# A two-layer decoder trunk on one core: halves for branch 0 and for the next layer made sooner, four p projections inside the first PLE gate tile, the first pair's head sums after half a matmul tile

## What is computed

```python
for i in range(DEPTH):                                   # DEPTH = 2
    xn = rmsnorm(h, norm_mix[i])
    q, k, v, cb, cc, cu, pu, gate_logits = split(xn @ w_in[i])
    att  = stick_breaking_attention(rmsnorm(q), rmsnorm(k), v)     # 8 heads x 64
    conv = cb * causal_short_conv(cc * cu, conv_w[i])
    pool = causal_pool_mixer(pu, pool_w[i]) * pool_scale[i]
    branch_d = einsum('bsjc,jcd->bsjd', stack([att, conv, pool]), w_branch[i])
    h = h + sum_j(sigmoid(gate_logits_j) * branch_d_j) @ w_out[i]
    h = h + peer_ffn(rmsnorm(h, norm_ffn[i]), ...)       # 16384 one-neuron experts, 8 heads x top 16
    h = h + sigmoid(rmsnorm(h, norm_ple[i]) @ w_ple_gate[i]) * (p[i] @ w_ple_proj[i])
```

## Time and profile before

| | us |
|---|---|
| runs | 3905.82, 3909.05, 3908.99 |
| median | 3908.99 |
| profiled execution, its own time | 3910.81 |
| span of that profile | 3909.0 |
| PE busy | 3828.8 (98% of the span) |
| DVE busy | 2878.5 (74%) |
| ACT busy | 1450.8 (37%) |
| POOL busy | 1474.3 (38%) |
| mean granted TensorE clock | 0.992 of full speed |

### The profile page before, as it was taken

One profiled execution on the slowest core, in us unless ns is written; L12 is line 12 of the kernel. 1 busy time (PEld: TensorE's weight loads), 2 busy tenths in 40 slices (PEclk: granted clock), 3 DMA queues, 4 the chain that ended last, 5 costly groups with the idle time before them and its releaser, 6 DMA issues.

```text
span 3909.0 us, 53929 instructions
## 1 busy us (share of the span) xinstructions
PE 3828.8 (98%) x17258; PEld 3140.4 (80%) x17258; DVE 2878.5 (74%) x4061; ACT 1450.8 (37%) x1957; POOL 1474.3 (38%) x935
## 2 busy tenths in 40 slices
PE   8999999999999999999999999999999999999997
PEld 5777888888888878888767778888888887888886
DVE  6753658989997287788577536599899963888785
ACT  5533333333333333333444333333333333333334
POOL 1100003444444277666101000045444443777651
PEclk9999999999999999999999999999999999999998
DMA  3222223445554699999222223234455546999991
GB/s 114 70 86 97 92 92 123 144 172 189 187 188 175 209 357 360 358 352 342 102 69 77 85 93 101 88 131 145 172 194 192 189 165 231 370 361 352 351 330 70
DMA packets 323770, 740.36 MB, mean 189 GB/s; under 512 B 30497, under 2 KB 161697, under 8 KB 319905
## 3 DMA queue, kind: packets, MB, share of 16 engines
q1 hardware_dynamic: 104400, 381.73, 28.1%
q10 hardware_dynamic: 174160, 222.40, 16.6%
q0 software_dynamic: 45056, 134.38, 9.3%
HBM read 618.87 MB, written 119.54 MB: 189 GB/s over the span
## 4 chain that ended last, share of the span: by engine, by line
PE 95%; DVE 2%; issue 1%; ACT 1%; DMA 1%; POOL 0%; DVEq 0%; ACTq 0%; POOLq 0%; SPq 0%
PE banks L1218 62%; PE banks L1434 26%; PE banks L1413 2%; PE banks L1280 1%; PE banks L1270 1%; PE banks L1288 1%; PE banks L1360 0%; ACT hi L453 0%; PE banks L1265 0%; DVE xl L787 0%; DMA vrow<-in_stream,tail_v 0%; DVE lo L775 0%; DMA raw<-in_stream 0%; ACT xh L469 0%; DVE xl L956 0%
## 5 line engine op out<-in xcount | busy, mean ns | idle before, releaser
L1218 PE MATMUL banks<-xh,hi 128*128 128x512 f32 x3264 | 1293.1, 396 | 27.1 <-DVE xl L787 18.5
L1218 PE MATMUL banks<-xl,hi 128*128 128x512 f32 x3264 | 1276.0, 391 | 0.0
L1218 PE MATMUL banks<-xh,lo 128*128 128x512 f32 x3264 | 1273.7, 390 | 0.0
L401 POOL TENSOR_TENSOR lo<-raw,hi 128x1024 fp32r<-128x1024 f32 x240 | 646.0, 2692 | 984.0 <-ACT hi L453 983.8
L775 DVE TENSOR_TENSOR lo<-raw,hi 128x1024 fp32r<-128x1024 f32 x484 | 586.6, 1212 | 418.2 <-ACT hi L453 351.7
L453 ACT ACTIVATE hi<-raw 128x1024 fp32r<-128x1024 f32 x724 | 739.5, 1042 | 261.3 <-DMA raw<-in_stream 162.6
L1218 PEld LDWEIGHTS banks<-xh,hi 128*128 128x128 f32 x3264 | 615.4, 189 | 166.0 <-DVE xl L787 23.6
L1218 PEld LDWEIGHTS banks<-xh,lo 128*128 128x128 f32 x3264 | 614.6, 188 | 130.9
L1218 PEld LDWEIGHTS banks<-xl,hi 128*128 128x128 f32 x3264 | 616.0, 189 | 122.4 <-issue 5.6
L1434 PE MATMUL banks<-hi,ah 128*128 128x512 f32 x1536 | 475.2, 391 | 13.2 <-issue 11.7
L1434 PE MATMUL banks<-lo,ah 128*128 128x512 f32 x1536 | 474.4, 390 | 0.0
(11 more groups left out here) (211 smaller groups left out, 3442.0 us busy)
## 6 DMA issues: line engine op xcount, KB each, us to landing
raw<-in_stream SPq DMA_DIRECT2D x724, 512.0 KB
early<-eo ACTq DMA_DIRECT2D x256, 256.0 KB, 2.4
gate_table<-stage ACTq DMA_DIRECT2D x24, 2048.0 KB, 7.1
...
```

Of the source, the lines that this page charges most:

```text
L401: pool.tensor_tensor(lo[k % RING][:, :], raw[k % RAW][:, :], hi[k % RING][:, :].bitcast(f32), ALU.subtract).then_inc(lo_split, 1)
L1218: ins = pe.matmul(out_ap, st[slot][:, a:a + P], mv, start=first and i == 0, stop=last and i == 2)
```

## The change

Four edits, in both layers:

1. Branch 0. The third gate block is taken out of the loops of ACT and DVE. `brh` of branch 0 is written before the sigmoid of the last gate tile, chunk by chunk as PE's last gate tile has read `xh`; `brl` before DVE scales that tile.
2. End of a layer. Only four projections go through `pj` (EARLY_PJ = 4). Projections 4 to 7 go into banks 1, 0, 7 and 3 (`late_bank`), are issued inside the first PLE gate tile, behind its chunks 1, 3 and 5, and DVE multiplies them out of PSUM. The squares of `hT` start sooner on ACT, and two splits stand later on DVE and ACT.
3. Next layer's halves. ACT rounds chunks 0 to 6 of `hT` around the sixth and seventh gate tile's sigmoid and no longer after two splits; DVE makes five of the low halves before and two after it scales the last tile. The last two splits stand behind the last square and the last low half.
4. First pair of a layer: `ssq(0)` stands behind the first half of the v tile and no longer ahead of it.

```diff
 A_U = NB * DC
+EARLY_PJ = 4
...
+def late_bank(m):
+    return bank[(1, 0, 7, 3)[m - EARLY_PJ]]
...
         apart(act)
-        with act.Fori(0, NB) as j:
+        def squash(j, m):
+            act.wait_ge(gate_scaled, 2 + l * (NB * DC) + j * DC + m + 1)
+            g = G3[:, bass.ds(j, 1), m, :].rearrange("p a t -> p (a t)")
+            act.activation(g, g, ACT.Sigmoid).then_inc(act_evac, 1)
+        with act.Fori(0, NB - 1) as j:
             for m in range(DC):
-                act.wait_ge(gate_scaled, 2 + l * (NB * DC) + j * DC + m + 1)
-                g = G3[:, bass.ds(j, 1), m, :].rearrange("p a t -> p (a t)")
-                act.activation(g, g, ACT.Sigmoid).then_inc(act_evac, 1)
+                squash(j, m)
                 split(l, N_GATE + m + AHEAD, j)
+        for m in range(DC - 1):
+            squash(NB - 1, m)
+            split(l, N_GATE + m + AHEAD, NB - 1)
+        for c in range(GROUPS):
+            act.wait_ge(x_read, l * X_READ + (NB - 1) * (DC - 1) + c + 1)
+            act.activation(brh[:, 0, c, :], BR[:, 0, c, :], ACT.Copy).then_inc(br_hi, 1)
+        squash(NB - 1, DC - 1)
+        split(l, N_GATE + DC - 1 + AHEAD, NB - 1)
...
                 act.wait_ge(tile_done, RING + l * T + N_BR + DC // 2)
-            for c in range(GROUPS):
-                if j == 0:
-                    act.wait_ge(x_read, l * X_READ + (NB - 1) * (DC - 1) + c + 1)
+            for c in range(GROUPS if j else 0):
...
-            if m < DC - 1:
-                act.wait_ge(v_out, l * (DC - 1) + m + 1)
-            else:
-                act.wait_ge(tile_done, RING + l * T + N_PLE)
+            act.wait_ge(v_out, l * EARLY_PJ + m + 1)
...
         take_pj(2)
+        square(l, 2, 0)
...
         added(4)
+        take_pj(3)
+        square(l, 2, 1)
         split(l, N_PT + 1 + AHEAD)
-        take_pj(3)
...
         added(6)
-        square(l, 2, 0)
-        square(l, 2, 1)
-        take_pj(4)
+        square(l, 2, 2)
+        square(l, 2, 3)
         added(7)
-        square(l, 2, 2)
+        for c in range(4, DC):
+            square(l, 2, c)
         split(l, N_PT + 2 + AHEAD)
-        take_pj(5)
-        square(l, 2, 3)
-        square(l, 2, 4)
-        take_pj(6)
-        square(l, 2, 5)
-        square(l, 2, 6)
-        take_pj(7)
-        square(l, 2, 7)
...
+        def reround(c):
+            act.wait_ge(x_read, l * X_READ + (NB + 1) * (DC - 1) + c + 1)
+            round_h(l + 1, 0, c)
         for m in range(DC):
-            if m == DC - 1:
-                split(l, N_PLE + m + AHEAD)
-                for c in range(DC - 1):
-                    act.wait_ge(x_read, l * X_READ + (NB + 1) * (DC - 1) + c + 1)
-                    round_h(l + 1, 0, c)
...
             act.activation(ge[:, m % 2, :], ge[:, m % 2, :], ACT.Sigmoid).then_inc(act_evac, 1)
-            if m < DC - 1:
+            if m < DC - 2:
                 split(l, N_PLE + m + AHEAD)
-            else:
+            if m == DC - 2:
+                for c in range(3):
+                    reround(c)
+            if m == DC - 1:
...
             square(l + 1, 0, m)
+            if m == DC - 2:
+                for c in range(3, DC - 1):
+                    reround(c)
+        for m in range(DC - 2, DC):
+            split(l, N_PLE + m + AHEAD)
...
             split(l, 11, b)
-        with dve.Fori(0, NB) as j:
+        def scale_gate(j, m):
+            dve.wait_ge(tile_done, RING + l * T + N_GATE + j * 8 + m + 1)
+            dve.tensor_tensor(G3[:, bass.ds(j, 1), m, :].rearrange("p a t -> p (a t)"), bank[4 + m % 2][:, :],
+                              rs[0][:, :], ALU.mult).then_inc(gate_scaled, 1)
+        with dve.Fori(0, NB - 1) as j:
             for m in range(DC):
-                dve.wait_ge(tile_done, RING + l * T + N_GATE + j * 8 + m + 1)
-                dve.tensor_tensor(G3[:, bass.ds(j, 1), m, :].rearrange("p a t -> p (a t)"), bank[4 + m % 2][:, :],
-                                  rs[0][:, :], ALU.mult).then_inc(gate_scaled, 1)
+                scale_gate(j, m)
...
-        dve.wait_ge(act_evac, 2 + l * A_ALL + NB * DC)
...
+        for m in range(DC - 1):
+            scale_gate(NB - 1, m)
+            split(l, N_GATE + m + AHEAD, NB - 1)
         branch_low(0)
+        scale_gate(NB - 1, DC - 1)
+        split(l, N_GATE + DC - 1 + AHEAD, NB - 1)
+        dve.wait_ge(act_evac, 2 + l * A_ALL + NB * DC)
...
         low_value(2)
-        split(l, N_PT + 1 + AHEAD)
...
         low_value(4)
+        split(l, N_PT + 1 + AHEAD)
...
         inverse(l, 2)
+        def low_next(c):
+            low_h(l + 1, 0, c, (l + 1) * (4 * DC))
...
             if m == DC - 1:
-                split(l, N_PLE + m + AHEAD)
-                for c in range(DC - 1):
-                    low_h(l + 1, 0, c, (l + 1) * (4 * DC))
+                for c in range(5):
+                    low_next(c)
...
             dve.tensor_tensor(ge[:, m % 2, :], bank[4 + m % 2][:, :], rs[2][:, :], ALU.mult).then_inc(ple_scaled, 1)
+            if m == DC - 1:
+                for c in range(5, DC - 1):
+                    low_next(c)
             dve.wait_ge(act_evac, 2 + l * A_ALL + A_PLE + m + 1)
-            link(dve.tensor_tensor(pj[:, m, :], pj[:, m, :], ge[:, m % 2, :], ALU.mult))
+            link(dve.tensor_tensor(pj[:, m, :], pj[:, m, :] if m < EARLY_PJ else late_bank(m)[:, :], ge[:, m % 2, :], ALU.mult))
             dve.tensor_tensor(hT[:, m, :], hT[:, m, :], pj[:, m, :], ALU.add).then_inc(ple_added, 1)
-            if m < DC - 1:
+            if m < DC - 2:
                 split(l, N_PLE + m + AHEAD)
-            else:
-                low_h(l + 1, 0, m, (l + 1) * (4 * DC))
+            if m == DC - 1:
+                low_next(m)
+        for m in range(DC - 2, DC):
+            split(l, N_PLE + m + AHEAD)
...
             mix(1, 1)
-            ssq(0)
+            if not first:
+                ssq(0)
             mix(2, 4, 0)
+            if first:
+                ssq(0)
+                mix(2, 4, 1)
...
             ssq(1)
-            mix(2, 4, 1)
+            if not first:
+                mix(2, 4, 1)
...
-            if m >= 2:
-                pe.wait_ge(pj_out, l * DC + m - 1)
+            if 2 <= m < EARLY_PJ:
+                pe.wait_ge(pj_out, l * EARLY_PJ + m - 1)
+            to = bank[6 + m % 2] if m < EARLY_PJ else late_bank(m)
...
                 pt, w = (N_PT + c) % RING, (N_PT + 2 + c) % RING
-                ins = three(bank[6 + m % 2][:, :], (w, m * P), hi[pt][:, 0:SEQ], lo[pt][:, 0:SEQ], c == 0, c == 1)
-            if m < DC - 1:
+                ins = three(to[:, :], (w, m * P), hi[pt][:, 0:SEQ], lo[pt][:, 0:SEQ], c == 0, c == 1)
+            if m < EARLY_PJ:
                 ins.then_inc(v_out, 1)
-            else:
+            if m == DC - 1:
...
         turn_values(6)
-        project(4)
         turn_values(7)
-        for m in range(5, DC):
-            project(m)
-        for m in range(DC):
+        pe.wait_ge(ple_scaled, l * DC + 1)
+        pe.wait_ge(lo_split, RAW + l * T + N_PLE + 1)
+        for c in range(DC):
+            if c == DC - 1:
+                pe.wait_ge(pj_out, (l + 1) * EARLY_PJ)
+                last_sums(l * 3 + 2)
+            pe.wait_ge(xl_ready, l * (4 * DC) + 3 * DC + c + 1)
+            ins = three(bank[4][:, :], (N_PLE % RING, c * P), xh[:, c, :], xl[:, c, :], c == 0, c == DC - 1)
+            if c == 1:
+                pe.wait_ge(dve_evac, 4 + l * V_ALL + V_ADD + 4)
+                project(4)
+            if c == 3:
+                pe.wait_ge(dve_evac, 4 + l * V_ALL + V_ADD + 7)
+                project(5)
+            if c == 5:
+                pe.wait_ge(pj_out, (l + 1) * EARLY_PJ)
+                project(6)
+                project(7)
+        ins.then_inc(tile_done, 1)
+        for m in range(1, DC):
             pe.wait_ge(ple_scaled, l * DC + m + 1)
-            if m == 0:
-                pe.wait_ge(pj_out, (l + 1) * DC)
-            dense(l, N_PLE + m, bank[4 + m % 2][:, :], (xh, xl),
-                  after=(xl_ready, l * (4 * DC) + 3 * DC) if m == 0 else None,
-                  late=l * 3 + 2 if m == 0 else None, signal=m == DC - 1)
+            dense(l, N_PLE + m, bank[4 + m % 2][:, :], (xh, xl), signal=m == DC - 1)
```

## The result

The changed kernel took **3880.41 us** (median of 6 runs, 3876.98 to 3885.17) where the kernel before took 3909.88 on the same chip (6 runs, 3905.82 to 3911.20): a ratio of 0.9927 with a 95% interval of 0.9914 to 0.9940. It is faster, as forecast, by 29.5 us and not by 38.4; 3880.4 lies 0.4 above the range and 9.8 above the predicted time. The profiled execution took 3879.68 (span 3877.9, granted clock 0.995 on average): 31.1 less than the profiled one of before.

The account below looks back on a forecast made before the run. The prediction took TensorE (PE) as the bound, 95% of the chain of waits. Its terms, 14.0 + 19.0 + 2.0 - 0.7 + 4.1 = 38.4 us, took the median from 3908.99 to 3870.6, range 3863 to 3880.

Parts of the forecast that it names:

- Branch 0: First branch tile: 4.45 us idle and 2.55 us of lost clock go, 7.0 per layer, 14.0 in all.
- End of a layer: Projections to `last_sums`: `last_sums` starts 9.5 us sooner per layer, 19.0 in all.
- The cover of 0.5 at chunk 5: First PLE gate tile: low half 5 done at 1898.0, PE at chunk 5 at 1898.5, so no wait.
- Next layer's start: Start of layer 1: `scores` 3.2 us sooner, behind a new 3.2 us PE wait; 2.0 net, once.
- about six matmuls at half clock, 1.2 us: Layer 1, behind the new wait before `scores`: the clock loss, suggested by a 2.71 us wait.
- First pair in layer 0: Moving `ssq(0)` behind half the v tile delays ACT's root and `kb`: 0.7 us lost, ends 0 and 1.5.
- End of the program: Layer 1's last addition, which releases the store, comes 4.1 us sooner (3.0 to 4.5).
- the new waits cost clock: Rival: four new idle places (`last_sums` twice, `scores` twice) cost twelve slow matmuls each; 8.8 us less gain, 3879.4; chance 0.11.
- The hand-overs are late: Rival: thin covers in branches, gate tile 2 and chunk 5 fail by 1 to 2 us each; 3877; chance 0.14.
- a sign of being wrong that the text had named: PE waiting for `dve_evac` or `xl` inside the first gate tile.
- Slower: Rival: clock stays at 1.2 GHz through gate tiles 1 to 7, 33.6 us per layer; 3938; chance 0.03.
- The slower rate of 1.65: Layer ends: all five POOL sums at 1.65 us; `last_sums` 1.0 later, total gain 1.9 us smaller.

Follow-up runs that it names:

- b3: Changed kernel plus nine useless matmuls ahead of PE's wait for `kb` in the first pair of each layer: 3873.54 us, ratio 0.9911 to the kernel before.
- a2_tail: Kernel before with only the layer-end part (projections inside the first PLE gate tile, matching order of squares and splits): 3890.66 us, ratio 0.9955.
- c1: Changed kernel with POOL's additions of squares on one column of 512 from the third square on, output wrong, for timing only: 3875.46 us, ratio 0.9914.
- b2: Changed kernel without the head sums' part, `ssq(0)` back ahead of the v tile: 3876.41 us, ratio 0.9917 to the kernel before.
- c2: Changed kernel plus nine useless matmuls before the `kb` wait, ACT's last two splits moved up, square-root table loaded at layer end: 3873.60 us, ratio 0.9910.

## Why the prediction was right and wrong

The signs and places of all but one term were right: both big waits are gone, and the first branch matmul, `last_sums` and the SQRT load are where the text said. Term by term, by the stages of the profiled executions, forecast against measured:

- **Branch 0: 14.0, measured 13.2.** 2 x 4.61 of idle time, and 2.65 and 1.30 behind it. The last of these holds a chance stretch at half clock in layer 1's query stage, which took 1.6. Without it the term would be 14.8; in b3, without it there, layer 1's two stages gave 8.6. So the working of the term held, with 0.8 more than it said, and that it came out below 14.0 is chance.
- **End of a layer: 19.0, measured 18.0.** The working took sums of 1.46 and low halves of 0.66. They took 1.64 and 1.22 to 1.53, since the change puts the two engines beside each other. Five sums of 0.18 more are 0.9, where the layers were 0.7 and 0.3 short. The cover of 0.5 at chunk 5 failed: the longer low halves made PE wait 0.7 there. That cost nothing further, because PE stood before POOL's sums for another 1.5; I had not worked this out, so it was luck.
- **Next layer's start: 2.0, measured -0.35.** `scores` came 2.9 sooner (forecast 3.2), with a wait for `kb` of 2.99 (3.2). The step that failed is "about six matmuls at half clock, 1.2 us": it cost 3.25. I had priced a wait of 3.2 by the row behind a wait of 2.71; the rows behind 4.45 were nearer in what they showed, 2.55. And layer 1 of the same trace, where I had not looked, has the same 2.71 us wait with half clock through the next projection too. PE's timeline of the kernel before:

```profile
3838.00 0.80 PE L1218 MATMUL banks<-hi,hi 128*128 128x512 f32 x1 [2.71 <-ACT pj L706]
...
3843.72 0.63 PE L1218 MATMUL banks<-hi,lo 128*128 128x512 f32 x1
```

- **First pair in layer 0: -0.7, measured -2.0.** Counted from the first sums over the partitions (28.01 in the changed kernel), `scores` came 0.7 later, as worked out: 22.7 in all six kernels with the move, 22.03 in the six without it. The start of the program up to those sums varies by itself, which makes the 0.38 of the table. But behind the wait, now 1.98 instead of 0.30, the clock fell and took 1.63. The sum had the wait and gave its clock no price; only the rival had one.
- **End of the program: 4.1, measured 2.3.** The last addition came 3.0 sooner, 45.1 behind `last_sums` instead of 48.1; low halves of 0.89 instead of 0.66 took 1.1 of it. From the addition's end to the end of the span it was 7.4 instead of 6.7; why is open.

The shortfalls are 0.8 + 1.0 + 2.35 + 1.3 + 1.8 = 7.3, the difference of 38.4 and 31.1. The other 2.5 of the 9.8 come from the step from profile to median: the profiled execution was 1.8 above the median before, and 0.7 below it in the changed kernel. What makes single runs differ is open. Runs of the changed kernel spread over 8 us, those of a2_tail over 1.3 (in fewer runs).

So of the rivals, "the new waits cost clock" was the truth in half of its four places: the two waits for `kb` cost 4.9 together, the two of 1.5 ahead of `last_sums` nothing (the matmul starts behind them stay 0.23 apart). "The hand-overs are late" happened once per layer, at chunk 5 (0.7 us, a sign of being wrong that the text had named), and cost nothing beside the wait that followed it. "Slower" named the right cause and the wrong size: the clock came back by itself before 1979. The slower rate of 1.65, which I had set beside the sum as 1.9 us smaller, gives 17.1 for the two ends of a layer together; the measured 18.0 lies halfway between it and the sum. It priced nothing on DVE, where the low halves cost 1.1 more at the end of the program and 1.1 ahead of `scores` of layer 1 (c1, in which both come 1.1 sooner, gives this back).

The sign of the head sums' part is the plainest lesson. I had found that it gains nothing, since `ssq(0)` comes no sooner. It does gain a little: `ssq` then runs at full clock (1.12 instead of 2.07 in b2), and `scores` comes 1.2 to 1.35 sooner. What I did not ask is what the wait costs where it now stands. Ahead of `ssq` most of the clock lost behind the wait is made good, because PE has slack until `kb` comes (in before it was 0.48 short); ahead of `scores` there is no slack behind it, and every slow matmul counts. That a filled wait keeps the clock is shown, in both layers of b3 and c2; what decides whether an unfilled one loses it is not.

The best kernels here are b3_warm and c2_preload, 3873.5 and 3873.6, 34.7 and 36.1 us below the kernel before that ran beside them.
